# The MLP's down projection in seven block products in place of eight, with the block sums on VectorE

## The reference, cut to what matters

```python
    h2 = rms_norm(x, ln_mlp_pre)
    ff = jnp.square(jax.nn.relu(h2 @ w_up)) @ w_down
    return x + rms_norm(ff, ln_mlp_post)
```

## Time and profile before

| | us |
|---|---|
| runs, median (lowest, highest) | 1902.52 (1901.78, 1903.50) |
| span of the profiled execution | 1901.8 |
| TensorE busy | 1881.2 |
| VectorE busy | 1140.6 |
| ScalarE busy | 491.9 |
| GpSimd busy | 350.8 |

### The profile page before, as it was taken

The page is one execution under the profiler, slowest core; times in us unless marked ns, Lnnn a source line. Parts: engine busy times, 40 slices in busy tenths (PEclk is TensorE's granted clock), DMA queues, the critical chain, the costliest instruction groups (busy, mean ns, idle before and its releaser), DMA issues.

```text
span 1901.8 us, 24979 instructions
## 1 busy us (share of the span) xinstructions
PE 1881.2 (99%) x8814; PEld 1525.0 (80%) x8814; DVE 1140.6 (60%) x1920; ACT 491.9 (26%) x967; POOL 350.8 (18%) x549
## 2 busy tenths in 40 slices
PE   8999999999999999999999999999999999999998
PEld 6877767888788888888878767678888888888887
DVE  5855789753476542453478558888434765325534
ACT  3163352421334100011221633524122331000101
POOL 2221111111220222222112211111112202222220
PEclk9999999999999999999999999999999999999999
DMA  6432123322521332222222321132225223222221
GB/s 240 137 123 83 67 67 97 84 67 78 202 98 45 122 100 99 90 99 100 78 89 89 133 72 67 67 99 71 78 78 220 68 78 101 98 100 100 90 98 56
DMA packets 73053, 186.78 MB, mean 98 GB/s; under 512 B 18368, under 2 KB 30848, under 8 KB 72064
## 3 DMA queue, kind: packets, MB, share of 16 engines
q1 hardware_dynamic: 41904, 152.10, 23.5%
q10 hardware_dynamic: 31056, 33.38, 5.2%
HBM read 174.40 MB, written 11.06 MB: 98 GB/s over the span
## 4 chain that ended last, share of the span: by engine, by line
PE 95%; ACT 2%; DVE 1%; issue 1%; DMA 0%; DVEq 0%; SPq 0%; ACTq 0%
PE psD L1099 24%; PE psD L1101 24%; PE psD L1100 24%; PE psM L1100 4%; PE psM L1101 4%; PE psM L1099 4%; PE psM L1158 2%; PE psM L1172 1%; PE psM L1367 1%; PE psM L1165 1%; PE psM L1385 1%; PE psM L1264 1%; PE psM L1373 1%; PE psM L1256 1%; ACT wide L1611 1%
## 5 line engine op out<-in xcount | busy, mean ns | idle before, releaser
L1099 PE MATMUL psD<-a_hi,w_hi 128*128 128x512 f32 (+2 forms) x1488 | 594.6, 400 | 0.8 <-DVE w_lo L1009 0.6
L1101 PE MATMUL psD<-a_hi,w_lo 128*128 128x512 f32 (+2 forms) x1488 | 575.2, 387 | 0.0
L1100 PE MATMUL psD<-a_lo,w_hi 128*128 128x512 f32 (+2 forms) x1488 | 574.2, 386 | 0.0
L1009 DVE TENSOR_TENSOR w_lo<-raw,w_hi 128x1024 fp32r<-128x1024 f32 x208 | 253.9, 1221 | 290.1 <-POOL w_hi L1077 289.4
L1099 PEld LDWEIGHTS psD<-a_hi,w_hi 128*128 128x128 f32 (+1 forms) x1488 | 279.1, 188 | 76.1 <-issue 21.3
L1076 POOL TENSOR_TENSOR w_hi<-raw,tabs 128x1 fp32r<-128x1 f32 x272 | 60.9, 224 | 1512.7 <-PE psD L1101 1288.4
L1100 PEld LDWEIGHTS psD<-a_lo,w_hi 128*128 128x128 f32 (+1 forms) x1488 | 279.4, 188 | 57.3 <-issue 4.3
L1101 PEld LDWEIGHTS psD<-a_hi,w_lo 128*128 128x128 f32 (+1 forms) x1488 | 278.8, 187 | 57.8 <-issue 0.2
L1077 POOL TENSOR_SCALAR w_hi<-raw 128x1023 fp32r<-128x1023 f32 x272 | 298.5, 1098 | 0.0
L1884 ACT CAST f_hi<-gt 128x512 f32 x64 | 39.8, 622 | 476.0 <-DVE gt L2321 470.7
L2318 DVE TENSOR_SCALAR gt<-psD 128x512 f32<-128x512 f32 x64 | 44.2, 691 | 133.0 <-PE psD L1101 133.0
(11 more groups left out here) (273 smaller groups left out, 2577.2 us busy)
## 6 DMA issues: line engine op xcount, KB each, us to landing
raw<-in_ws SPq DMA_DIRECT2D x272, 512.0 KB, 3.2
s_raw<-in_wo ACTq DMA_DIRECT2D x14, 512.0 KB, 11.5
x<-rows_d ACTq DMA_DIRECT2D x4, 1024.0 KB, 5.6
x<-out ACTq DMA_DIRECT2D x2, 2048.0 KB, 8.0
e_raw<-in_wo ACTq DMA_DIRECT2D x8, 512.0 KB, 6.6
tabs<-in_tab SPq DMA_DIRECT2D x1, 2944.0 KB, 11.5
x<-in_x SPq DMA_DIRECT2D x4, 512.0 KB, 6.7
out<-x SPq DMA_DIRECT2D x4, 512.0 KB, 7.5
```

The source lines that it names most:

```text
L1009: dve.tensor_tensor(w_lo[:, s, :], raw[:, s, :], w_hi[:, s, :].bitcast(F32), ALU.subtract) \
L1099: pe.matmul(out, lhi, rhi, start=start, stop=False)
L1100: pe.matmul(out, lhi, rlo, start=False, stop=False)
L1101: return pe.matmul(out, llo, rhi, start=False, stop=stop)
```

## The change

The down projection becomes a product of 2 × 2 blocks: tokens in halves of 256, hidden channels in halves, output channels in halves of 512. With A the activations and b the down weights, the sums are S1 = A21 + A22, S3 = A11 − A21, S2 = S1 − A11, S4 = A12 − S2 and T1 = b12 − b11, T2 = b22 − T1, T3, T4 as further differences, made in place in `d_raw`. Seven products take the place of eight: A11·b11, A12·b21, S1·T1, S2·T2, S4·b22, S3·T3 and A22·T4 (`PRODUCTS`; the third entry names the PSUM banks).

The MLP is worked in four chunks of 8 hidden tiles. A chunk has 8 up slabs of 24 matmuls as before, and 14 steps (`STEPS`: each product for two pairs of hidden tiles) of 2 × 2 × 3 = 12 matmuls: per layer 4 × 14 × 12 = 672. A step's weights (`d_hi`, `d_lo`) lie in one of RING = 3 buffers.

- ScalarE does ReLU and square, rounds f in two parts (A: three blocks, 768 elements; B: four, 1024), rounds the up slabs (`round_up`) and the operands of the steps (`d_high`).
- VectorE does the sums of activations (`combine`, 256 elements), the sums of weights (`made`, 1024), f_lo (`f_rest`), d_lo (`d_rest`), w_lo, and 16 evictions per chunk (512 each), which add or subtract into `wide`.
- SyncE loads `d_raw` on the same queue as the up slabs, and its loop is written out. The tables (`tabs`) share memory with what the MLP now needs and are partly loaded again for the second layer.
- The last chunk does six steps whole and the other eight tile by tile (`ending`), first P6 and P3 for tiles 0 and 1, then P7 and P4 for tiles 2 and 3. `e_raw` and the eight held slabs are gone.
- GpSimd keeps the rounding of the mixer's slabs and of the next layer's first two.

The core of the diff:

```diff
+PRODUCTS = {"P1": (A11, "b11", "X"), "P2": (A12, "b21", "Y"), "P5": (S1, "b12", "Z"), "P6": (S2, "b12", "X"),
+            "P3": (S4, "b22", "Z"), "P7": (S3, "b11", "X"), "P4": (A22, "b21", "V")}
+STEPS = [("P1", 0), ("P2", 0), ("P1", 1), ("P2", 1), ("P5", 0), ("P5", 1), ("P6", 0), ("P6", 1), ("P3", 0), ("P3", 1),
+         ("P7", 0), ("P7", 1), ("P4", 0), ("P4", 1)]
...
+WHOLE = 6
+RING = 3
...
+        banks = {"X": psM[0:2], "Y": psM[2:4], "Z": psD[0:2], "V": psD[2:4]}
...
+                    for m in range(0 if layer else 2, NSLAB):
...
+                            sp.wait_ge(*on("split", m + 1))
+                            sp.dma_start(raw[:, n % 2, :], ws[n]).then_inc(sem(f"raw_in{n % 2}"), 16)
...
+                        if m >= SL_MLP:
+                            c, k = divmod(m - SL_MLP, CT)
...
+                            elif c:
+                                b, j = list(DOWN_SLOT)[k]
...
+                                sp.wait_ge(*on("d_lo", (c - 1) * NSTEP + last_step + 1))
...
+                            sp.dma_start(d_raw[:, k, :], wd[layer * len(DOWN) + c * CT + k]).then_inc(*inc("d_in" + WITH[k][0], 16))
...
+                    def down(c, st):
+                        if st == 0:
+                            pe.wait_ge(*on("evict", 16 * (c - 1) + 14) if c else on("a_lo", (2 + ST) * KT))
...
+                        if st in (6, 8, 10):
+                            pe.wait_ge(*on("evict", 16 * c + {6: 2, 8: 6, 10: 8}[st]))
...
+                        operands_in(c, st)
+                        for tt in range(2):
+                            ins = product(c, st, tt)
+                        ins.then_inc(*inc("d_done"))
...
+                    def ending(c):
+                        for t in range(ST):
+                            for q in (("P6", "P3") if t < 2 else ("P7", "P4")):
+                                if q == "P4":
+                                    pe.wait_ge(*on("relu_up", c * CT + 8))
+                                else:
+                                    pe.wait_ge(*on("evict", 16 * c + {"P6": 2, "P3": 5 + t, "P7": 3 + 2 * t}[q]))
                                 for j in range(2):
...
+                            down(c, st)
+                    ending(CHUNKS - 1)
...
+                    def relu(c, i):
+                        act.wait_ge(*on("slab_done", SL_MLP + c * CT + i + 1))
+                        if i % 2 == 0 and c * CT + i:
+                            act.wait_ge(*on("f_loB", (c * CT + i) // 2))
...
+                        sig(act.activation(f_pair(i), psD[i % 4][:].rearrange("p (a s) -> p a s", a=2), ACT.Relu), "relu_up")
+                        own("relu_up")
+                        sig(act.activation(f_pair(i), f_pair(i), ACT.Square), "f_sq")
...
+                    def round_up(c, i):
...
+                        if n < NSLAB:
+                            s = (layer * NSLAB + n) % 2
+                            act.wait_ge(*on("w_hi", n))
+                            act.wait_ge(*on("slab_done", n - 1))
+                            act.wait_ge(sem(f"raw_in{s}"), 16 * ((layer * NSLAB + n) // 2 + 1))
+                            act.copy(w_hi[:, s, :], raw[:, s, :]).then_inc(sem("w_hi"), 1)
...
+                    def f_halves(c, p, part):
...
+                        if part == "A":
+                            own("f_sq")
+                        else:
+                            act.wait_ge(*on("comb", 4 * (c * PAIRS + p + 1)))
+                        sig(act.copy(f_hi[:, p, w, :], fr[:, w, :]), "f_hi" + part)
+                    def d_high(c, st):
+                        q, j = STEPS[st]
+                        if (q, j) in MADE:
+                            act.wait_ge(*on("T", c * CT + MADE[q, j]))
+                        else:
+                            act.wait_ge(*on(*landed_at(c, DOWN_SLOT[PRODUCTS[q][1], j])))
+                        operand_free(act, c, st)
+                        sig(act.copy(operand(c, st)[0], source(st)), "d_hi")
...
+                    for c in range(CHUNKS):
+                        for i in range(CT):
+                            if i % 2 == 0:
+                                round_up(c, i)
+                            relu(c, i)
+                            if i % 2:
+                                f_halves(c, i // 2, "A")
+                                round_up(c, i)
+                                f_halves(c, i // 2, "B")
+                            elif i:
+                                d_high(c, i // 2 - 1)
+                        for st in range(RING, NSTEP if c < CHUNKS - 1 else 10):
+                            d_high(c, st)
+                            if c == CHUNKS - 1 and st == 7:
+                                for t in range(2):
...
+                    for st in (10, 11, 12):
+                        d_high(c, st)
                     for t in range(ST):
+                        if t < 2:
+                            halves2(t, 1, 8 + 2 * t)
+                            if t:
+                                d_high(c, 13)
+                        else:
+                            halves2(t, 1, 3 * t + 5)
+                            halves2(t, 0, 3 * t + 7)
...
+                    def combine(c, p, to, left, right, op):
+                        if to in (S1, S3):
+                            dve.wait_ge(*on("f_sq", c * CT + 2 * p + 2))
+                        else:
+                            own("comb")
+                        sig(dve.tensor_tensor(fr[:, to, :], fr[:, left, :], fr[:, right, :], op), "comb")
+                    def made(c, b, j, split, minus):
+                        to, left, right = (d_raw[:, DOWN_SLOT[n, j], :] for n in (b, *minus))
+                        for n in {b, *minus}:
+                            dve.wait_ge(*on(*landed_at(c, DOWN_SLOT[n, j])))
+                        if split:
+                            dve.wait_ge(*on("d_lo", c * NSTEP + STEPS.index((split, j)) + 1))
+                        if "T" in seen:
+                            own("T")
+                        sig(dve.tensor_tensor(to, left, right, ALU.subtract), "T")
...
+                    def f_rest(c, p, part):
...
+                        dve.wait_ge(*on("f_hi" + part, c * PAIRS + p + 1))
+                        sig(dve.tensor_tensor(f_lo[:, p, w, :], fr[:, w, :], f32(f_hi[:, p, w, :]), ALU.subtract), "f_lo" + part)
+                    def d_rest(c, st):
+                        hi, lo = operand(c, st)
+                        dve.wait_ge(*on("d_hi", c * NSTEP + st + 1))
+                        operand_free(dve, c, st)
+                        sig(dve.tensor_tensor(lo, source(st), f32(hi), ALU.subtract), "d_lo")
...
+                    def evict(t, half, bank, first=False, minus=False):
+                        w, ps = wide[:, t, half * S:(half + 1) * S], banks[bank][t % 2][:, :]
+                        if first:
+                            sig(dve.tensor_copy(w, ps), "evict")
+                        else:
+                            if "evict" in seen:
+                                own("evict")
+                            sig(dve.tensor_tensor(w, w, ps, ALU.subtract if minus else ALU.add), "evict")
...
+                    AFTER = {2: "P1", 3: "P2", 5: "P5", 7: "P6", 9: "P3", 11: "P7", 13: "P4"}
+                    THEN = {1: (t2, 0), 2: (t2, 1), 4: (t3, 0), 6: (t3, 1), 8: (t4, 0), 9: (t4, 1)}
+                    for c in range(CHUNKS):
+                        for i in range(CT):
+                            if i % 2 == 0:
+                                ahead(c, i)
+                                if i:
+                                    d_rest(c, i // 2 - 1)
+                                if i == 6:
+                                    t1(c, 0)
+                                continue
+                            p = i // 2
+                            combine(c, p, S1, A21, A22, ALU.add)
+                            combine(c, p, S3, A11, A21, ALU.subtract)
+                            f_rest(c, p, "A")
+                            if i < CT - 1:
+                                ahead(c, i)
+                            else:
+                                t1(c, 1)
+                            combine(c, p, S2, S1, A11, ALU.subtract)
+                            combine(c, p, S4, A12, S2, ALU.subtract)
+                            if i == CT - 1:
+                                d_rest(c, RING)
+                            f_rest(c, p, "B")
+                        ahead(c, CT - 1)
+                        for st in range(NSTEP if c < CHUNKS - 1 else WHOLE):
+                            if st in AFTER:
+                                dve.wait_ge(*on("d_done", c * NSTEP + st + 1))
+                                evict_product(c, AFTER[st])
+                            if st and st + RING < NSTEP:
+                                d_rest(c, st + RING)
+                            if st in THEN:
+                                THEN[st][0](c, THEN[st][1])
```

(56 more changed lines are left out.)

362 lines of the change are left out of this document (174 added, 188 removed).

## The result

The changed kernel takes 1913.03 us (median of four runs, 1912.04 to 1913.28) against 1902.76 for the kernel before, which ran beside it: 1.0054 times as long, 95% interval 1.0040 to 1.0068. It is slower by 0.54%, 10.3 us; the forecast was 1911.5, +9. The two profiled spans stand 8.3 apart and not 10.3 (a run's time is its span plus 1.8 to 1.9 us, in both kernels; the profiled execution of before lies at the upper end of its runs, that of the change is its quickest).

What follows compares the result with a forecast made beforehand. TensorE's matmul count was taken to bound the kernel. Saving 21.8 us per layer against stalls and tails gave +7.0 and +1.0, with +1 for second waits: 1902.5 + 9 = 1911.5 us, range 1898 to 1925.

Steps and rivals of the forecast that it cites:

- What goes: MLP down projection: 768 matmuls per layer become 672, saving 21.8 us per layer, 43.6 in all, the only gain.
- The head of each down phase: First steps after the eighth up slab: TensorE waits for VectorE's late d_lo at steps 3 to 6, 3.3 us per chunk.
- The walk: Queues followed in program order, each instruction starting at the later of its engine's pitch and its last wait.
- The ending: Last chunk's tile-by-tile steps: TensorE stalls 2.0, 4.0 and 2.1 us for d_lo 8, 11 and 13, 8.1 per layer.
- clock rival: Down-phase stalls lower TensorE's clock, eight spells adding 14 us: 1925 us; the ending's fall would be swallowed; chance 0.08.
- The tail: After TensorE's last MLP slot to the last diagonal: 15.3 and 7.1 us, +7.6 and +2.7; 8.45 us per tile.
- The sign that was given for it: Between the layers: 15 us from the last down matmul to layer two's first.
- Second waits: VectorE queue entries of 0.021 us: nothing if hidden, 1 us a layer if exposed; half taken, +1.
- The transfers: Added 512 KB loads on SyncE's queue with the up slabs: 0 taken, +2.4 us a layer at the slower rate.
- The sum: Whole kernel: first layer +7.0, second +1.0, second waits +1, together +9 us, giving 1911.5.
- the rival that VectorE keeps up: Also "the faster rival": a shorter pitch of VectorE's two-source instructions removes most stalls, −30, 1872 us; chance 0.18.
- the one that it empties between instructions: VectorE's pitch grows to 1.22 and 0.69 us without overlap, 5.2 us more per layer, 1922 us; chance 0.05.

Runs made afterwards that it cites:

- ninth experiment: Changed kernel with VectorE's and ScalarE's queues reordered at down-phase heads and ending, tile 1's diagonal earlier, next layer's first two slabs rounded on ScalarE: 1876.78 us.
- third experiment: Changed kernel with the up slabs rounded on GpSimd again, as before the change: span 1915.6 us against 1910.1.
- experiments 1: Changed kernel with VectorE's w_lo for the next up slab moved behind step 7, in the last chunk behind the last sum: span 1903.7 us against 1910.1.
- 4: Changed kernel with the eight sums of weights per chunk moved from VectorE to GpSimd: 1937.69 us, 1.0185 times the kernel before.
- 5: Changed kernel with the next layer's first two slabs rounded on ScalarE instead of GpSimd: span 1909.7 us against 1910.1.
- experiments 2: Changed kernel with evictions that add into the sums cut to 8 of 512 columns, output incomplete: span 1888.4 us against 1910.1.
- 6: Changed kernel, down-phase heads reordered: T1's second half earlier, step 3's d_hi ahead of f_hi B, w_lo later: span 1888.1 us against 1910.1.

## Why the prediction was right, point by point

*What goes.* Right: 96 matmuls per layer at 0.2269. In the ninth experiment, with the waits away, TensorE's stretch from the first full-width matmul to the last is 317.4 us (613.56 to 930.98), against 337.34 less 21.8 = 315.6.

*The head of each down phase.* Right in cause and size: 3.3 us a chunk forecast; 3.2, 3.3, 3.3 and 4.2 measured in the first layer, 3.2, 3.3, 3.3 and 2.3 in the second, the sum of the losses behind 0.1. Each of the four waits came at its step. The walk's 0.62 at step 3 was 0.44, the least exact of the four; its 0.67 at step 4 was 0.60, its 1.01s 0.99 and 1.07 (0.87 and 1.04 in the first layer's first chunk). The 4.2 holds GpSimd's 0.9.

*The ending.* Waits of 2.0, 4.0 and 2.1 forecast; 1.9, 4.0 and 0.4 to 0.5 measured, and the sum is 8 all the same, since the matmuls between the second and the third ran at half pace. The granted clock's row:

```profile
940.00:944.00 4.00, 4.00 (x12) 3.11 (x12) 3.04 (x5) 1.97 (x5) 0.00 (x0) 0.61 0.33 131
```

That is the clock rival's own sentence, a fall behind the 4 us pause that the next wait swallows. In the down phases the granted clock stood at 1.00 (738 to 752 us) through all four waits, so the rest of that rival fell. By the Trainium skill, TensorE: Matmul & The Clock Gate, section "HAM oscillation — how this bites in real kernels", the ending alone qualified; the trace agrees.

*The tail.* +7.6 and +2.7 forecast, +6.9 and +2.9 measured, on the loop that was named: a tile each 8.2 us (954.09, 962.25 are the starts of the additions to x) against 8.45. The sign that was given for it, 15 us to layer two's first matmul, left out the turning of the last tile: to the last diagonal it is 14.6, to that matmul (968.40) 17.1 from the last one's start.

*The bounds.* Second waits were taken at +1 for both layers, 0.5 each: the stretches came 1.8 and 1.1 over the walk, 0.9 of the first GpSimd's. Whether the rest is second waits was not tried. The transfers were taken at 0, and no DMA stands in the chain that ended last; ScalarE's d_hi waited 3.7 us for a landing, over all chunks together.

*The sum* is in part luck. The two MLPs came 2.1 us over the walk with its allowance, and the other four stretches 2.7 under their forecasts, so that +9 met +8.4.

*VectorE's pitch.* It stayed: d_lo and the sums at 1222 and 1221 ns, the next one 1.13 to 1.15 after. With it fell the rival that VectorE keeps up and the one that it empties between instructions. That the next one is listed ahead of a listed end doesn't show, as the prediction has it, that the trace contradicts the rule quoted there: no run shows when the pipeline is empty.

*One step of the reasoning was wrong,* though nothing hung on it here: against the faster rival stood that w_lo takes 1221 ns "with GpSimd at work" and 1220 without. GpSimd had finished its rounding when w_lo ran, since w_lo waits for it. Four of the eight e_lo did run beside a rounding, but had started ahead of it; there the sign stood in GpSimd's row, 2.05 us where its mean is 1.10, in the trace of before:

```profile
867.36 4.63 DVE L2378 TENSOR_TENSOR e_lo<-e_raw,e_hi 128x1024 fp32r<-128x1024 f32 x4
...
870.87 2.05 POOL L1077 TENSOR_SCALAR w_hi<-raw 128x1023 fp32r<-128x1023 f32 x1
```

The third experiment shows that the two do slow each other, and that the roundings' move to ScalarE, which the prediction put off the chain on either engine and costed at nothing, is worth 5.5 us. Without it the spans would have stood 14 us apart, not 8. The prediction also put the median of the runs 0.7 above the profiled execution of before; that was a time against a span. The difference of +9 does not depend on it.

*Not forecast:* the 1.4 us won back between the layers (below), and the first MLP starting 0.8 us earlier. The latter tells nothing: in the changed kernel and the nine of the experiments, which do the same up to there, that start lies between 612.40 and 613.56.

## What to carry to other kernels

When a change takes work off the bounding engine and gives other work to one that is free on average, look at what falls between two hand-overs and in which order: here 36 us hung on the order in the queues of VectorE and ScalarE (about 1 us of it on the two roundings), and a walk through those queues with pitches from the old trace found the four waits of a down phase to 0.2 us, three of them to 0.1. Put into a queue first what someone waits for next, push what is needed late (here w_lo and the tiles' gains) behind it, and do ahead, where the queue has room, what would stand in the way later (T1's second half). An idle engine is no free place before the trace shows the two of them working at the same moment.

## What the runs showed of the hardware

- VectorE and GpSimd slow each other when VectorE's instruction reads two operands from the chip's memory: d_lo 1222 to 1954 ns on average, a 1024-element subtraction on GpSimd 2.40 to 3.17 us; evictions from PSUM unmoved at 684 ns. The one that starts later pays: a VectorE sum begun 0.09 us ahead of a rounding kept its 1.22 us, the rounding took 2.05.
- TensorE's granted clock can fall where it costs nothing. Before, it fell behind the first layer's tail, when TensorE had full work again (0.57). After, the tail is longer, the low stretch lies in it, and the clock is back when the work is:

```profile
954.50:961.50 7.00, 4.76 (x22) 4.76 (x23) 4.74 (x11) 3.40 (x10) 0.00 (x0) 0.51 0.52 209
966.00:970.00 4.00, 3.66 (x23) 2.97 (x24) 2.70 (x6) 3.22 (x6) 0.00 (x0) 1.00 0.30 118
```

  No run was made for it alone, but the kept traces fall into two groups by it. Where the low stretch ends ahead of the last diagonal (the changed kernel and experiments 1, 3, 4, 5 and 9), 597.2 to 597.3 us pass from that diagonal to the second MLP. Where it comes behind it (the kernel before and experiments 2 and 6), 598.6 us pass. The 1.4 us of the table are this difference.
